# A hybrid attention and pooling block on 8 cores: decay products on GpSimd, and g of six chunk pairs by seven products in place of eight

## What is computed

```python
h = jnp.einsum('bsd,de->bse', x, w_in)
q, k, v, g, a_low, u, z, gate_a, gate_b = jnp.split(h, SPLIT_POINTS, axis=-1)
# per chunk, with b = cumulative log decay inside the chunk:
o_inter = einsum('bhck,bhkv->bhcv', qi * exp(b), state)
scores  = einsum('bhik,bhjk,bhijk->bhij', qi, ki, decay)
new_state = exp(b_last) * state + einsum('bhck,bhcv->bhkv', ki * exp(b_last - b), vi)
y_a = rms_norm_heads(o, gn_w) * silu(g)
```

## Time and profile before

| | us |
|---|---|
| median of 3 runs | 585.55 (584.23, 585.55, 587.86) |
| the profiled execution | 584.62 |
| its span, slowest core | 583.1 |
| span of the fastest core | 581.2 |

### The profile page before, as it was taken

One profiled execution on the slowest core, in us unless ns is written; L12 is line 12 of the kernel. 1 busy time (PEld: TensorE's weight loads), 2 busy tenths in 40 slices (PEclk: granted clock), 3 DMA queues, 4 the chain that ended last, 5 costly groups with the idle time before them and its releaser, 6 DMA issues.

```text
span 583.1 us, 10349 instructions; the slowest of 8 cores (581.2 to 583.1 us)
## 1 busy us (share of the span) xinstructions
PE 566.3 (97%) x2990; PEld 279.7 (48%) x2990; DVE 441.9 (76%) x841; ACT 290.4 (50%) x619; POOL 113.4 (19%) x184
## 2 busy tenths in 40 slices
PE   6899999999999999999999999999999999999993
PEld 2344445555555655444444444444444455555562
DVE  2478988888777797887877888466785577788786
ACT  2479965666666676454232333657633244322223
POOL 1020003454454360000101000100000023314331
PEclk9999999999999999999999999999999999999998
DMA  8999944167374617813217104894401424444442
GB/s 217 322 182 168 166 86 90 58 113 126 73 113 85 92 37 119 117 22 52 21 16 87 23 0 67 131 162 75 73 2 37 138 79 146 135 154 144 143 149 110
DMA packets 48008, 60.21 MB, mean 103 GB/s; under 512 B 30864, under 2 KB 36624, under 8 KB 45648
## 3 DMA queue, kind: packets, MB, share of 16 engines
q0 software_dynamic: 7184, 21.50, 24.1%
q1 hardware_dynamic: 36304, 33.97, 22.6%
q10 hardware_dynamic: 4464, 4.08, 2.8%
HBM read 61.10 MB, written 14.16 MB: 129 GB/s over the span
## 4 chain that ended last, share of the span: by engine, by line
PE 91%; DVE 3%; DMA 2%; issue 1%; SPq 1%; ACT 1%; POOL 1%; DVEq 0%; ACTq 0%; POOLq 0%
PE pb L951 27%; PE pb L1045 14%; PE pb L679 9%; PE pb L1628 8%; PE pb L712 8%; PE pb L409 5%; PE pb L1513 4%; PE pb L429 4%; PE pb L1553 2%; PE pb L1499 2%; DMA A<-head 2%; PE pb L764 1%; PE pb L769 1%; PE pb L781 1%; SPq L306 1%
## 5 line engine op out<-in xcount | busy, mean ns | idle before, releaser
L1045 PE MATMUL pb<-A,ws 128*128 128x512 bf16 x256 | 64.1, 379 | 0.0
L679 PE MATMUL pb<-A,xT 128*128 128x512 bf16 x256 | 62.4, 379 | 0.2 <-ACT A L673 0.2
L951 PE MATMUL pb<-A,ws 128*128 128x512 bf16 x216 | 53.1, 379 | 0.0
L956 ACT COPY sgm_t<-pb 128x512 f32<-128x512 f32 x54 | 31.7, 586 | 27.2 <-PE pb L951 26.4
L1646 ACT ACTIVATE wg_s<-xT 128x512 bf16<-128x512 f32 (+1 forms) x32 | 19.9, 623 | 49.0 <-DVE xT L1637 48.6
L951 PE MATMUL pb<-xT,ws 128*128 128x512 bf16 x172 | 44.2, 379 | 0.0
L804 POOL TENSOR_SCALAR A<-A,eblast 128x256 bf16<-128x256 f32 x30 | 29.7, 990 | 66.3 <-ACT A L805 39.3
L1666 POOL TENSOR_SCALAR small<-small 128x1 f32<-128x1 f32 x15 | 19.3, 1285 | 119.8 <-DVE small L1661 119.8
L1045 PEld LDWEIGHTS pb<-A,ws 128*128 128x128 bf16 x256 | 25.0, 98 | 30.2
L1022 ACT ACTIVATE sgm_t<-sgm_t 128x512 f32<-128x512 f32 x24 | 15.1, 630 | 48.0 <-DVE sgm_t L982 24.8
L259 POOL DMA_DIRECT2D ws<-wts x10 | 5.5, 548 | 168.6 <-PE pb L951 82.7
(11 more groups left out here) (207 smaller groups left out, 1178.3 us busy)
## 6 DMA issues: line engine op xcount, KB each, us to landing
ws<-wts POOLq DMA_DIRECT2D x10, 1024.0 KB, 10.7
A<-head SPq DMA_DIRECT2D x32, 256.0 KB, 9.7
A<-x SPq DMA_DIRECT2D x16, 512.0 KB, 5.3
out<-xT SPq DMA_DIRECT2D x15, 512.0 KB, 4.1
A<-wts POOLq DMA_DIRECT2D x7, 1024.0 KB, 26.7
yscr<-A ACTq DMA_DIRECT2D x29, 128.0 KB, 2.7
kscr<-A SPq DMA_DIRECT2D x12, 128.0 KB, 2.6
xT<-xt POOLq DMA_DIRECT2D x2, 512.0 KB, 11.2
```

Source lines behind the costliest of these rows:

```text
L679: PE(lambda e, k=k: e.matmul(pb[bank][:, :], xTc(c, k), W.ap[:, k, :], start=(k == 0), stop=(k == KC - 1)), r=[W.b], w=[bb[bank]])
L951: PE(lambda e, k=k: e.matmul(pb[bank][:, :], u(k), x(k), start=first and k == 0, stop=k == 3, skip_group_check=True), r=[ub] + xb, w=[bb[b ...
L956: ACT(lambda e: e.copy(SG[s], pb[bank][:, :]), r=[bb[bank]], w=[b_SG[s]])
L1045: PE(lambda e, k=k: e.matmul(pb[bank][:, :], W.ap[:, k, m * 128:(m + 1) * 128], aT[:, k, tb * 512:(tb + 1) * 512], start=(k == 0), stop=(k ...
```

## The change

Five things change together.

- `finalize_one` gets an engine. Token blocks 1 and 2 and heads 0 and 1 of block 3 go to POOL, in the projection loop at p = 1, 2, 5, 6 and 7 (ten units, 20 operations); block 0 stays on DVE in the projections; heads 2 and 3 of block 3 go to DVE in steps 14 and 15.
- g of pairs 2 to 7 is made by `gq(1, pair, i)`: seven products with bB = 7, sharing banks 3 and 4, the GU sums and the GT buffers with v. Product 4 comes one period later. The silu of products 3 and 1 is held back in `g_wait` until the next product 2 or 0.
- The sums of g's weights (`gv_sums(1)`) are made on DVE in steps 0 to 5, most of them as two halves. GU sums 3 and 4 of pairs 2 to 7 go to POOL.
- `u0` is loaded at step 12 to the place of q and k of block 0; R[0] and R[1] hold g's weight sums and GT meanwhile. `kd` moves to A4.
- `wp_part` of block 0 moves from steps 25 to 27 to steps 27 and 28, its banks change, and the sums of x for u start at step 27 (both there).

```diff
-        def finalize_one(tb, h):
+        def finalize_one(tb, h, eng=None):
...
-            DVE(lambda e: e.tensor_tensor(qbT[:, h, sl], qbT[:, h, sl], EpT[:, h, sl], ALU.mult),
+            ENG = eng or DVE
+            ENG(lambda e: e.tensor_tensor(qbT[:, h, sl], qbT[:, h, sl], EpT[:, h, sl], ALU.mult),
                 r=[b_EpT[u]], w=[b_qbb[h][tb]])
-            DVE(lambda e: e.tensor_tensor(kbT[:, h, sl], kbT[:, h, sl], EmT[:, h, sl], ALU.mult),
+            ENG(lambda e: e.tensor_tensor(kbT[:, h, sl], kbT[:, h, sl], EmT[:, h, sl], ALU.mult),
                 r=[b_EmT[u]], w=[b_kbb[h][tb]])
...
+        FIN_AT = {1: ((1, 0), (1, 1)), 2: ((1, 2), (1, 3)), 5: ((2, 0), (2, 1)), 6: ((2, 2), (2, 3)), 7: ((3, 0), (3, 1))}
...
             gate_cum(p)
+            for tb, h in FIN_AT.get(p, ()):
+                finalize_one(tb, h, POOL)
...
-        fin_pending += [(tb, h) for tb in range(1, 4) for h in range(4)]
...
-        kd = [R1f[:, 0:1024], R1f[:, 1024:2048]]
+        kd = [A4[:, 0:1024], A4[:, 1024:2048]]
...
-            UENG(lambda e: e.tensor_tensor(GU[i], a, b, op), w=[b_GU[i]])
+            (POOL if pair > 1 and i in (3, 4) else DVE)(lambda e: e.tensor_tensor(GU[i], a, b, op), w=[b_GU[i]])
+
+        g_wait = []
...
             elif i in (2, 0):
+                while g_wait:
+                    g_wait.pop(0)()
                 t = 2 if i == 2 else 1
...
                 if kind:
-                    vg_evac(1, c, blk, GT[t], [b_GT[t]])
+                    g_wait.append(lambda: vg_evac(1, c, blk, GT[t], [b_GT[t]]))
...
-            bks = (0, 1) * 4 if blk else (7, 4, 3, 4, 7, 4, 7, 4)
+            bks = (0, 1) * 4 if blk else (2, 2, 3, 4, 2, 3, 0, 4)
...
-        wu = [R[0], Wt(A4[:, 0:4096].rearrange("p (k n) -> p k n", k=KC), "wu1")]
+        wu = [Wt(A1[:].rearrange("p (k t) -> p k t", k=KC)[:, :, 0:512], "wu0"), Wt(A4[:, 0:4096].rearrange("p (k n) -> p k n", k=KC), "wu1")]
...
+        GV_AT = [[(0, 0), (0, 1)], [(1, 0), (1, 1)], [(2, 0), (2, 1)], [(3, 0)], [(4, 1), (5, 0)]]
...
             n, c = 4 * (pair - 1), 2 * pair
+            if pair > 1:
+                for j, units in enumerate(((5, 2) if pair > 2 else (5,), () if pair > 2 else (2,), (0, 6), (15, 3, 1), (), (12, 4), (10, 16), (13, 11))):
+                    for u in units:
+                        put(n + j // 2, j % 2, gq, u // 10, pair, u % 10)
+                put(n + 4, 1, gq, 1, pair, 4)
...
-        for n, pos, f, args in ((25, 1, wp_part, (0, 0, 1)), (26, 0, wp_part, (0, 1, 2)), (26, 1, wp_part, (0, 2, 4)),
-                                (27, 0, wp_part, (0, 4, 6)), (27, 1, wp_part, (0, 6, 8)), (28, 0, direct_u, (0, 0)), (28, 1, direct_u, (0, 1)),
...
+        for n, pos, f, args in ((27, 0, wp_part, (0, 0, 1)), (27, 1, wp_part, (0, 1, 3)), (28, 0, wp_part, (0, 3, 7)),
+                                (28, 1, flush_g, ()), (28, 1, wp_part, (0, 7, 8)), (28, 1, direct_u, (0, 0)),
...
-        ld(R[0], "u0", extra=readers(b_wq))
...
-        tail_ops = {26: [xs1[0]], 27: [xs1[1]]}
+        tail_ops = {27: [xs1[0], xs1[1]]}
...
-            drain_fin({0: 3, 1: 2, 2: 1, 5: 1, 7: 1, 8: 1, 10: 1, 11: 1, 12: 1, 13: 1, 15: 1}.get(n, 0))
+            for h in {14: (2,), 15: (3,)}.get(n, ()):
+                finalize_one(3, h)
...
-            if n // 4 + 2 < NT // 2:
-                for u in {1: (2, 0), 2: (6, 3), 3: (4,)}.get(n % 4, ()):
+            if n % 4 > 1 and n // 4 + 2 < NT // 2:
+                for u in {2: (2,), 3: (0, 3, 6)}[n % 4]:
                     gu_sum(u, n // 4 + 2)
+            if n % 4 == 0 and 0 < n // 4 + 1 < NT // 2 and n:
+                gu_sum(4, n // 4 + 1)
+            if n == 12:
+                ld(wu[0], "u0", extra=lastops([b[0] for b in b_qbb + b_kbb]))
```

More of the change, by code:

```diff
@@ L597, in tt, with f @@
             def tt(i, a, b, op, r):
-                def f():
+                def f(h=slice(0, 4)):
                     vb[i].r = vb[i].r + ex.get(i, [])
-                    DVE(lambda e: e.tensor_tensor(V[i] if i != 3 else b21, a, b, op), r=r, w=[vb[i]])
+                    o = V[i] if i != 3 else b21
+                    DVE(lambda e: e.tensor_tensor(o[:, h], a[:, h], b[:, h], op), r=r, w=[vb[i]])
                 return f
@@ L603, in gv_sums @@
                     tt(1, V[0], b12, ALU.subtract, [vb[0], W1.b]),
-                    lambda: DVE(lambda e: e.tensor_scalar(V[0], V[0], -1.0, None, ALU.mult), w=[vb[0]]),
+                    lambda h=slice(0, 4): DVE(lambda e: e.tensor_scalar(V[0][:, h], V[0][:, h], -1.0, None, ALU.mult), w=[vb[0]]),
                     tt(3, b22, b21, ALU.subtract, [W0.b, W1.b])]
@@ L754, in kd_block @@
                    r=[b_kbb[h][0], b_ident], w=[bb[bank]])
-            DVE(lambda e: e.tensor_copy(kd[i], pbT[bank][:, 0:1024]), r=[bb[bank]], w=[b_kds[i]])
+            DVE(lambda e: e.tensor_copy(kd[i], pbT[bank][:, 0:1024]), r=[bb[bank]], w=[b_kds[i]], extra=lastops(b_la))
         def st_UO1(n):
@@ L1071, in wp_part @@
             W = wp[blk]
-            bks = (0, 1) * 4 if blk else (7, 4, 3, 4, 7, 4, 7, 4)
-            uW = wu[blk].ap.rearrange("p (c a) n -> p c (a n)", c=4)
+            bks = (0, 1) * 4 if blk else (2, 2, 3, 4, 2, 3, 0, 4)
             for k in range(k0, k1):
@@ L1163, in build_program @@
             n, c = 4 * (pair - 1), 2 * pair
+            if pair > 1:
[3 more added lines that the diff above has]
+                put(n + 4, 1, gq, 1, pair, 4)
+                if pair == NT // 2 - 1:
+                    flush_g = lambda: [g_wait.pop(0)() for _ in range(2)]
+                continue
             g = {a + h: (proj_g, c + i // 2, i % 2, (7, 3)[i % 2], j)
@@ L1168, in build_program @@
                     put(n + j // 2, j % 2, *(g[u] if isinstance(u, str) else (gq, 0, pair, u)))
+        for i, pos in enumerate(GV_AT):
+            for h in (slice(0, 2), slice(2, 4)) if i != 3 else (slice(0, 4),):
+                put(*pos.pop(0), lambda i=i, h=h: gv_sums(1)[i](h))
         def direct_u(p, half):
@@ L1253, in build_program @@
             if n == 19:
-                ld(wu[1], "u1", extra=lastops(b_kT[0:8]))
+                ld(wu[1], "u1", extra=lastops(b_kT[0:8] + b_kds))
             if n == 28:
                 POOL(lambda e: e.memset(mask_t[:], 1.0), w=[b_ones], extra=[P.last["pe"]])
-            if n in (26, 27):
-                for b in b_V[1][n % 2 * 2:n % 2 * 2 + 2]:
-                    b.r = [P.last["pe"]]
+            if n in (27, 28):
+                for i in {27: (0, 1, 3), 28: (2,)}[n]:
+                    b_V[1][i].r = [P.last["pe"]]
             on_dve(tail_ops.get(n, ()))
```

9 lines of the change are left out of this document (5 added, 4 removed).

## The result

The changed kernel took 594.65 us (median of four runs, 593.36 to 595.22). The kernel before, run beside it, takes 585.55 us without its one disturbed run, and the ratio of the undisturbed runs is **1.0147**, with a 95% interval of [1.0101, 1.0193]. 581.7 us with a range of 579.0 to 587.5 was predicted; the rival "the hold lasts as long as POOL's instruction" had been priced at 595 us and given a chance of 0.08.

A forecast was written before the change was run, and what follows sets the result against it. PE's matmul count was taken to bound the chunk stage, with PE only just ahead in the projections. 584.62 - 5.18 + 0.5 + 0.5 + 0.3 = 580.7, plus 0.93 to the runs' median: 581.7 us, range 579.0 to 587.5.

The forecast's parts named there:

- the hold lasts as long as POOL's instruction: Projections: DVE's scans queue behind POOL's decay products and PE waits near 80 us; +14 us, 595 us in all; chance 0.08.
- Term 3: Projections: 20 decay products on POOL beside a full DVE hold it up only briefly; +0.5 us, bounds 0 and 14.
- Term 2: Chunk stage: g's extra reading-out fits; the subtraction frees product 2's bank about 0.2 us in time; +0.5 us, bounds 0 and 4.
- Term 1: Chunk stage, pairs 2 to 7: 24 fewer wide matmuls on PE, all on the path; -5.18 us, period 15.16 us.
- Term 4: End of projections: g's second weight half lands late as sends of k share the DMA engines; +0.3 us, bounds 0 and 3.9.
- The tail: Stretches after 204 us: nothing was put there; a change of more than 2 us would mean the prediction was wrong altogether.
- the full hold: Projections: POOL's decay products hold DVE for their whole length; +14 us, 595 us in all; chance 0.08.
- The late subtraction: Chunk stage, period ends: DVE's subtraction frees product 2's bank late each period; +4 us for +0.5, 585.1 us; chance 0.09.

## Why the prediction was wrong, step by step

- **Term 3, the products on POOL: the step that failed.** "So POOL holds DVE up in its first third of a microsecond and not for its length" was drawn from the earlier trace rows, where POOL's operation is a scaled copy with one tensor input. The products have two, and beside them a DVE operation with two SBUF inputs waits for the end. 0.5 us was taken; the part alone cost 10.5 us (1.0185), within the bounds of 0 to 14 us. The nearest row was of another form, and its short hold was carried over as if the form didn't matter. The reading of that row was right: the changed kernel shows such a copy hold DVE for a third of a microsecond (last section). With the longer hold scans of 1.22 us took 1.73, DVE came about 9 us late to v's sums, and PE stood still for 4.24 us ahead of v's product 2. That the upper bound of 14 us lies near the result is in part luck: a product takes 1.15 us and not 1.86, and ten of these less 4.6 would give 6.9 us.
- The rule of the Trainium skill that was set against the row ("SBUF — State Buffer", section "SBUF: two separate sides") is what this trace shows for the products. For the one-input copy of the earlier trace rows rule and measurement differ: a DVE product begun 0.34 us into its 0.93 us was not delayed, and the measurement decides.
- **The granted clock fell behind PE's long wait**, which no term had. Behind the 4.24 us of standing still the granted clock of the slowest core was 0.50, the level of 1.2 GHz, for 88 to 92 us and 0.72 on the mean of the next four (second and third row, in the columns of the earlier trace rows); from 96 us it was back at 1.00. At 3.34 and 4.00 us of work that is some 2.8 us more, an estimate from these rows, and part of the 11.1. All eight cores of the change show such a stretch, behind waits of 4.2 to 5.7 us, and so does the run with the products alone (5.7 us); the kernel before and the runs with the products back on DVE and with fills, where PE has no such wait, show none there. One thing stays open: on cores 4 to 7 the clock was lower already before the wait (first row: 0.81 with PE busy throughout), on cores 0 to 3 it was not.

```profile
72.00:76.00 4.00, 4.00 (x17) 1.68 (x16) 3.90 (x3) 1.20 (x2) 4.00 (x4) 0.81 0.63 126
...
88.00:92.00 4.00, 3.34 (x19) 2.04 (x20) 3.60 (x7) 2.41 (x6) 0.00 (x0) 0.50 0.66 94
92.00:96.00 4.00, 4.00 (x19) 1.81 (x18) 1.38 (x2) 0.81 (x2) 0.00 (x0) 0.72 0.55 103
96.00:100.00 4.00, 4.00 (x20) 1.54 (x18) 3.30 (x8) 1.30 (x3) 0.00 (x0) 1.00 0.02 4
```

- **Term 2, the extra reading-out: mis-sized.** 0.5 us was taken, with an upper bound of 4; the chunk stage lost about 4.5. PE's waits there, by the starts of its matmuls, come to 5.5 us against 1.0 before: 2.3 us ahead of v's product 2, in six places; 1.4 at 115 to 118 us, near the weight sums; 0.5 for a copy on ACT; and the rest, most of it at the end of the stage. So the place was right for half of it: PE waits for the subtraction ahead of product 2. What the margin of 0.2 us left out is that y itself waits, 0.4 to 0.8 us, for what POOL and ACT make of the step, with the subtraction queued behind it. Rows of one step without that wait were taken for all. The first period of seven products costs more than the others, near the weight sums of g, and this was not foreseen; what PE waits for there stays open in part. One count was off too: twelve units, not eleven, stood in the steps, so ten left DVE.
- **Term 1 was right**: 24 matmuls fewer (2990 to 2966). A period of 15.16 us was expected; v's product 1 starts at 138.32 and 153.77 us, 15.45 us apart, with one wait of 0.29 us in between; other periods took up to 16.15.
- **Term 4** took 0.3 us and none shows: no matmul waited for a transfer. The fills on POOL, with the same sends of k at the same places, are the better test, and cost nothing.
- **The tail** gained 1.0 us on the slowest cores (0.4 by the medians of the eight) where nothing was put; `u0` and `wp_part` hurt nothing that the trace shows.
- Of the rivals, the full hold came true with its place and sign; its cost is 10.5 us and not 14. The late subtraction came with it, and took most of the 5.2 us that the rival's sum still subtracts in full. That this sum, 595 us, lies at the measured 594.65 is luck: the two errors nearly cancel.

## What to carry to other kernels

Before work goes to GpSimd, list what VectorE does in those microseconds by where its inputs lie. Beside GpSimd products of two tensors, operations with one input in PSUM ran undisturbed here (0.69 us as ever), those with two in SBUF waited nearly to the end of GpSimd's instruction, and cutting it up paid a fixed cost for each piece. A fill disturbed nothing, and a copy with one input held VectorE for a third of its length. So a row of another form is a hint and not a price. Where PE waits for one VectorE operation in every period, look first at what that operation is queued behind: letting it pass one that waits brought 2.1 us, while every change that moved matmuls between steps gained nothing or cost up to 11.
